# Attention products turned from features to tokens: exponentials split in two fp32r parts, attention stage unrolled

## What is computed

```python
def _fox_prompt_attention(q, k, v, logf):
    ...
        s = jnp.einsum('bqhd,bkhd->bhqk', q_i, k).astype(jnp.float32) * ATTN_SCALE
        s = s + cq_i[..., :, None] - ck[:, :, None, :]
        ...
        p = jax.nn.softmax(jnp.where(mask, s, -jnp.inf), axis=-1)
        return jnp.einsum('bhqk,bkhd->bqhd', p.astype(v.dtype), v)
...
            q, k_p, v_p, g, logf_p = _fox_project(yp, norm1_g, w_in1, fox_b_f, q_norm_g, k_norm_g)
            att = _fox_prompt_attention(q, k_p, v_p, logf_p)
            yp = yp + (att * jax.nn.silu(g)) @ w_out1
```

## Time and profile before

| | us |
|---|---|
| median of three runs | 3478.22 (3470.8 to 3479.21) |
| the profiled execution | 3480.33 |
| its span from first to last instruction | 3478.7 |
| PE busy, share of the span | 3017.1 (87%) |
| DVE / ACT / POOL busy | 1533.7 / 1032.3 / 761.5 |

### The profile page before, as it was taken

One profiled execution on the slowest core, in us unless ns is written; L12 is line 12 of the kernel. 1 busy time (PEld: TensorE's weight loads), 2 busy tenths in 40 slices (PEclk: granted clock), 3 DMA queues, 4 the chain that ended last, 5 costly groups with the idle time before them and its releaser, 6 DMA issues. The chain is left out here.

```text
span 3478.7 us, 48124 instructions
## 1 busy us (share of the span) xinstructions
PE 3017.1 (87%) x17005; PEld 2320.1 (67%) x17005; DVE 1533.7 (44%) x2068; ACT 1032.3 (30%) x1711; POOL 761.5 (22%) x475
## 2 busy tenths in 40 slices
PE   3879797959989999989996689898989889899799
PEld 3869696947759999989886445454545445454687
DVE  5132323233557667685775334343424333342332
ACT  5222223232452122221211234343434343343100
POOL 0000000010004886878765200000100000000000
PEclk9989898979989999999998799999999999999899
DMA  3111000035636888888785765748475757654442
GB/s 113 32 35 39 25 30 25 24 101 178 184 115 210 271 267 276 265 260 269 252 271 159 167 183 137 205 114 250 99 228 127 215 150 200 173 143 152 149 127 68
DMA packets 323904, 547.04 MB, mean 157 GB/s; under 512 B 77309, under 2 KB 221345, under 8 KB 314220
## 3 DMA queue, kind: packets, MB, share of 16 engines
q1 hardware_dynamic: 220172, 445.81, 42.8%
q10 hardware_dynamic: 95424, 75.61, 7.6%
q0 software_dynamic: 8128, 23.33, 2.1%
HBM read 449.58 MB, written 95.12 MB: 157 GB/s over the span
## 5 line engine op out<-in xcount | busy, mean ns | idle before, releaser
L1151 POOL TENSOR_TENSOR p_kp<-p_kp,p_qb 128x1024 f32<-128x1024 f32 x256 | 625.7, 2471 | 385.7 <-DMA p_kp<-in_cache_k_dram 314.0
L2076 DVE TENSOR_REDUCE at_mx<-at_mx 128x1 f32<-128x512 f32 (+3 forms) x640 | 379.9, 608 | 718.3 <-PE at_mx L1953 475.7
L2040 ACT ACTIVATE at_w<-at_st,c_nckt 128x512 f32<-128x512 f32 (+3 forms) x640 | 397.3, 623 | 690.9 <-PE at_st L1977 380.2
L1990 PE MATMUL at_o<-at_w,at_v 128*65 128x512 f32 (+3 forms) x1280 | 578.0, 535 | 17.0 <-DVE at_og L2086 8.0
L112 PE MATMUL p_pb<-p_w,x_xh 128*128 128x256 f32 x2048 | 591.8, 289 | 0.7 <-DVE p_w L1462 0.7
L113 PE MATMUL p_pb<-p_w,x_xh 128*128 128x256 f32 x2048 | 579.1, 283 | 0.0
L114 PE MATMUL p_pb<-p_w,x_xl 128*128 128x256 f32 x2048 | 578.6, 283 | 0.0
L1975 PE MATMUL at_st<-at_q,at_k 128*128 128x512 f32 (+3 forms) x640 | 407.4, 637 | 4.4 <-ACT at_w L2040 4.4
L1564 DVE TENSOR_REDUCE p_sc<-p_kp 128x16 f32<-128x1024 f32 x256 | 307.5, 1214 | 217.6 <-POOL p_kp L1151 217.3
L112 PEld LDWEIGHTS p_pb<-p_w,x_xh 128*128 128x128 f32 x2048 | 390.5, 191 | 12.1 <-issue 11.2
L113 PEld LDWEIGHTS p_pb<-p_w,x_xh 128*128 128x128 f32 x2048 | 391.9, 191 | 0.0
(11 more groups left out here) (289 smaller groups left out, 3880.4 us busy)
## 6 DMA issues: line engine op xcount, KB each, us to landing
p_kp<-in_cache_k_dram SPq DMA_DIRECT2D x256, 512.0 KB, 4.9
at_vp<-in_cache_v_dram SPq DMA_DIRECT2D x256, 512.0 KB, 5.6
o_mt<-mixed SPq DMA_DIRECT2D x32, 512.0 KB, 5.1
p_raw<-in_w_in_dram SPq DMA_DIRECT2D x32, 512.0 KB, 6.9
at_q<-qh SPq DMA_DIRECT2D x32, 512.0 KB
at_k<-kh SPq DMA_DIRECT2D x32, 512.0 KB
l_raw<-in_w_in_dram SPq DMA_DIRECT2D x20, 512.0 KB
mixed<-l_w POOLq DMA_DIRECT2D x8, 1028.0 KB, 4.2
```

Source lines behind the costliest of these rows:

```text
L1151: nc.gpsimd.tensor_tensor(kp[:, g % 4], kp[:, g % 4], qb[:], ALU.mult).then_inc(kmul, 1)
L1990: nc.tensor.matmul(O[0:HR, P * j:512], V[s][:, kb, :], W[n % 3][:, 0:512 - P * j], start=(kb == 0), stop=(kb == 4 * c + 3)).then_inc(pv, 1)
L2040: nc.scalar.activation(W[n % 3][:, 0:wd], ST[n % 2][:, 0:wd], ACT.Exp, bias=C.nckt[:, kb, ds(2 * i + u // NC, 1)]).then_inc(ex, 1)
L2076: nc.vector.reduce_max(mx[:, u % 2, j, seg:seg + 1], MX[m % 2][:, 0:wd], AX.X).then_inc(mread, 1)
```

## The change

1. In `attention` PV is turned: the exponentials become the stationary side, in tiles of 128 keys by 128 queries, and the values the moving side. Both are split in a high and a low fp32r part. For each tile there are two products: the high part with 130 columns (`V` high, two columns of ones, `V` low), and the low part with the first 66. At a unit's start a product with a row of zeros clears each half of `o`.
2. Between exponential and PV ACT rounds `w` to `wh` (RD), and POOL in two steps of three, DVE in the third, subtract for `wl` (WL). PV stands three steps behind its QK, further at a unit's start. `w` has four buffers, `wh` and `wl` five. The values of a head are split by ACT and POOL (VS).
3. The result lies by tokens. OE is on DVE alone, in two halves: reciprocal, four multiplications with division and gate, an addition. SP stores it; the gate is loaded by tokens, for each unit.
4. The maxima row goes through the `mx` tiles; `mr` is gone. The loop is gone: all 640 steps are written out, and waits are for constants.
5. In `project1` the gate isn't turned but stored by tokens, and the turn of a unit comes after the second next unit, `turn(n - 2)`.
6. In `out1` the division is gone; PE turns the tile of tokens by eight transposes, and ACT and DVE split it from PSUM.

```diff
             def turn(n):
...
-                if n and UNITS[n - 1][2] != "v":
-                    turn(n - 1)
+                if n >= 2 and UNITS[n - 2][2] in "qk":
+                    turn(n - 2)
...
+    VW = 2 * HD + 2
+    LAG = 3
+    RW, RH = 4, 5
...
+    def low_on_dve(n):
+        return n % 3 == 2
...
+        for h in range(2, H):
+            start = first_step(NC * (h - 1)) + 2
+            for x in range(NLD):
+                loads.setdefault(start + x, []).append(("LD", h, x))
+            loads.setdefault(start + NLD, []).append(("LV", h))
+            loads.setdefault(start + NLD + 9, []).append(("VS", h))
...
+            for x in range(NLD):
+                head_load(0, x)
             sp.dma_start(pt[:], a["page_table"]...).then_inc(pt_in, 16)
+            value_load(0)
+            gate_load(0)
+            gate_load(1)
             scores(0)
             sp.wait_ge(snz, 1)
             sp.dma_start(sn[0:1], ...).then_inc(sn_in, 16)
+            for x in range(NLD):
+                head_load(1, x)
+            sp.wait_ge(pt_in, 16)
+            value_group(0, 0)
+            value_group(0, 1)
+            value_load(1)
...
+            def value_low(h):
+                pool.wait_ge(vhd, h + 1)
+                nc.gpsimd.tensor_tensor(V[h % 2][:, :, LO], Vr[:], V[h % 2][:, :, HI].bitcast(F32), ALU.subtract).then_inc(vld, 1)
...
-                        nc.tensor.matmul(O[0:HR, P * j:512], V[s][:, kb, :], W[n % 3][:, 0:512 - P * j],
-                                         start=(kb == 0), stop=(kb == 4 * c + 3)).then_inc(pv, 1)
+                    for jj in range(j, 4):
+                        if kb == 0 and u and jj % 2 == 0:
+                            pe.wait_ge(osc, 2 * u - 1 + jj // 2)
+                        if kb == 0 and jj % 2 == 0:
+                            nc.tensor.matmul(O[:, jj // 2, 0:2 * VW], identr[0:1, :], zero[:], start=True, stop=False)
+                        q = slice(P * (jj - j), P * (jj - j + 1))
+                        nc.tensor.matmul(o_tile(jj, ALL), Wh[n % RH][:, q], V[s][:, kb, ALL], start=False, stop=False)
+                        last = nc.tensor.matmul(o_tile(jj, FRONT), Wl[n % RH][:, q], V[s][:, kb, FRONT], start=False,
+                                                stop=jj % 2 == 1 and kb == 4 * c + jj)
...
+            def value_high(h):
+                act.wait_ge(vr_in, 16 * (h + 1))
+                if h >= 2:
+                    act.wait_ge(pv, first_step(NC * (h - 1)))
+                nc.scalar.activation(V[h % 2][:, :, HI], Vr[:], ACT.Copy).then_inc(vhd, 1)
+
+            value_high(0)
+            value_high(1)
...
+                    nc.vector.reciprocal(ol[:, u % 2, 2 * half:2 * half + 2], one).then_inc(old, 1)
...
+                    for part, dst in ((HI, oa), (LO, ob)):
+                        for j in js:
+                            last = nc.vector.scalar_tensor_tensor(out=dst[:, j, :], in0=o_tile(j, part), scalar=ol[:, u % 2, j:j + 1],
+                                                                  in1=SG[u % 2][:, j, :], op0=ALU.mult, op1=ALU.mult)
+                    last.then_inc(osc, 1)
...
-                    last = nc.tensor.matmul(rb[:, n % 2, k, 0:rows], expand[:, k * P:(k + 1) * P], rl[:, ds(col, rows)],
-                                            start=True, stop=True)
+                    last = nc.tensor.transpose(tp[:, n % 2, k, :], mt[:, n % 3, k * P:(k + 1) * P], C.ident[:])
```

More of the change, by code:

```diff
@@ L1680, in attention, with blocks, first_step, width @@
     HR = HD + 1
-    NS = 2 * sum(4 * (c + 1) for c in range(NC))
-    NLD = 10
+    U = H * NC
+    HB = 2 * (NC * (NC + 1))
+    N = HB * H
+    NLD = 8
     VG = PG // 4
-    VI = PG // 4 + 1
+    VW = 2 * HD + 2
+    LAG = 3
+    RW, RH = 4, 5
+    def blocks(u):
+        return 4 * (u % NC + 1)
+    def first_step(u):
+        return HB * (u // NC) + sum(blocks(x) for x in range(u % NC))
+    def width(n):
+        u = max(x for x in range(NC * (n // HB), NC * (n // HB) + NC) if first_step(x) <= n)
+        kb = n - first_step(u)
+        return 512 - P * max(0, kb - 4 * (u % NC))
@@ L1848, in value_group, with values @@
                     page(vp[:, r % 2, g], a["cache_v"], PG * b + 4 * r + g).then_inc(v_in[r % 2], 16)
[L1850 to L1855 removed]
+            def values(b, r):
+                sp.wait_ge(vdone, (VG + 1) * b + r + 1)
                 if r < VG - 2:
@@ L1875, in _ @@
-            run(0, schedule(False), True, False)
-            with sp.Fori(1, B - 1) as i:
-                run(i, schedule(False), False, False)
-            run(B - 1, schedule(True), False, True)
+            due = []
+            for w in SEQ:
+                if w[0] == "LD":
+                    head_load(w[1], w[2])
+                elif w[0] == "LV":
+                    value_load(w[1])
+                elif w[0] == "OE" and w[2] == 1:
+                    due.append([3, w[1]])
+                elif w[0] == "SD" and w[-1] < B - 1:
+                    sp.wait_ge(sdd, 2 * w[-1] + 2)
+                    scores(w[-1] + 1)
+                elif w[0] == "VG":
+                    values(w[-1], w[1])
+                elif w[0] == "VN":
+                    values(w[-1], VG)
+                elif w[0] == "QK":
+                    for d in due:
+                        d[0] -= 1
+                    while due and due[0][0] <= 0:
+                        u = due.pop(0)[1]
+                        store(u)
+                        if u + 2 < U:
+                            gate_load(u + 2)
@@ L2159, in out1, with by_feature @@
         block = ctx.enter_context(nc.Block())
+        def by_feature(n, rows):
+            return tp[:, n % 2, :, :] if rows == P else ms[:]
         @block.sync
```

785 lines of the change are left out of this document (400 added, 385 removed).

## The result

| | before | after |
|---|---|---|
| median | 3477.53 us (4 runs) | 4064.57 us (4 runs, 4039.69 to 4078.92) |
| ratio, with its 95% interval | | 1.1685 (1.1625 to 1.1745) |
| the profiled execution | 3480.33 | 4078.92 |

What follows compares the result with a forecast made beforehand. PE was taken to bound attention, its clock falling to 1.2 GHz in even heads. 3480.3 + 461 (eight pairs) + 32 (start) + 3 (end) - 37 (project1) - 24 (out1) = 3915 us, range 3540 to 4010.

Steps and rivals of the forecast that it cites:

- PV's price: Attention: 0.11 us a product, 0.22 a tile at full clock, loads setting the price; +26 us at full clock.
- faster: Rival: loads overlap and a PV product costs less than 0.11 us; below 0.093 the kernel is faster; chance 0.05.
- Even heads: Attention: clock falls in unit c = 0 and stays at 1.2 GHz; 119.5 us a head, +53.6.
- Odd heads: Attention: groups of values bring the clock back each time; +4 us a head (0 to 12).
- the last chain: End of attention: the last blocks pass one more chain of exponential, rounding and subtraction; +3 us.
- the odd heads stay low too: Rival: a group of values at the low clock doesn't bring it back; 33 us more each, 4170; chance 0.08.
- The clock returns in part: Rival: clock returns by c = 1's steps or for half of the even heads; about 3700 us; chance 0.15.
- Project1: project1: 32 gate turns go, -13 us, and waits for a turn's rows shrink; -37 us in all (-13 to -50).
- The start: Start of attention: loads and the split of head 1's values delay the first QK to about 1992; +32 us (10 to 45).
- Out1: out1: inversion, spread and division go, eight transposes a tile come; -24 us.
- The chain: Attention: exponential, rounding, subtraction and hand-overs behind QK, some 4.3 us over three steps; 2.5 us a head at full clock.
- The clock stays up: Rival: c = 0 costs only one low stretch as before, a busy queue restoring the clock; 3552 us; chance 0.18.

Runs made afterwards that it cites:

- a5_low_130: Changed kernel with all 130 columns instead of 66 in the second product of each PV tile, no further load: 4033.62 us.
- e1_no_values: Changed kernel with seven of the eight groups of page values of each sample cut to one product of 8 columns: 4121.36 us.
- d2: Changed kernel with all but the first four pages of cached keys in project1 loaded with 128 of 1024 columns: project1 927.9 us, whole kernel 4077.86.
- d4: Changed kernel with GpSimd's multiplications of cached keys cut from 1024 columns to 64: project1 835.4 us, whole kernel 3978.67.
- a4: Changed kernel with the split of head 1's values on ScalarE and GpSimd moved from the stage's start to step 12: 4013.21 us.
- d3: Kernel before the change with GpSimd's multiplications of cached keys cut from 1024 columns to 64: project1 861.2 us, whole kernel 3429.15.
- a1_rows128: Changed kernel with operands of the second score product and the maxima product filled from 65 rows to 128: 3784.68 us.

## Why the prediction was wrong in size

**PV's price: right.** 0.22 and 0.44 us a tile were forecast from the earlier trace rows, 0.22 and 0.43 measured; a5_low_130 shows that the load is what counts. With this the rival "faster", which needed products under 0.093 us, falls.

**Even heads: right in size, wrong in place.** 123.9 instead of 119.5 us, low from end to end, as forecast. But the prediction let the clock fall in unit c = 0, while PE waits for VectorE. Unit c = 0 took 9.3 us, forecast 9.5, and that is luck: the forecast was VectorE's time with PE waiting and under 5 us of its own work. In head 4 PE was busy 9.30 of 9.30 us with this work at the low clock, since the clock had fallen earlier. Windows of the changed kernel: unit c = 0 of head 4, a stretch in head 7, then the end of head 7 up to the first QK of head 8:

```profile
2447.20:2456.50 9.30, 9.30 (x36) 8.59 (x36) 5.74 (x19) 3.53 (x8) 3.52 (x3) 0.50 0.49 106
...
2842.70:2852.90 10.20, 10.20 (x46) 6.99 (x44) 1.98 (x3) 1.98 (x4) 2.78 (x2) 0.50 1.02 290
...
2873.40:2893.90 20.50, 20.25 (x151) 14.96 (x143) 9.56 (x26) 11.73 (x22) 8.24 (x9) 1.00 0.59 186
2893.90:2904.10 10.20, 9.68 (x27) 6.24 (x28) 1.54 (x3) 1.21 (x2) 1.50 (x1) 0.50 0.50 161
2904.10:2917.80 13.70, 13.54 (x105) 12.52 (x104) 4.73 (x7) 9.89 (x17) 6.50 (x5) 1.00 0.46 154
2917.80:2922.10 4.30, 4.30 (x22) 4.30 (x22) 0.64 (x2) 1.79 (x5) 1.91 (x2) 0.50 0.09 19
```

Before the last fall PE was busy 13.54 of 13.70 us, with the new PV and the scores, and no wait above 0.2 us. So the plain stream loses the clock by itself. Heads 1, 3 and 9 end in the same way: PE busy for at least 13.4 us of 13.6 to 13.7 at 1.00, and then the fall.

**Odd heads: the step that failed.** "Groups of values ... bring the clock back each time" was true (e1_no_values), but the prediction took it that the clock then stays. Between groups and after the last one the plain stream loses it again, as in the rows above, and the clock is low for a time even where a group runs: the stretch from 2842.70 to 2852.90 holds 16 records of one. The odd heads ran at 0.68 to 0.83. They grew by 15.8 us each instead of 4, 94 us more in all and the largest part of the miss; the even ones by 58.2 instead of 53.6 (37 us). Less the 3 us booked for the last chain, that is the stage's 128. The profiled execution was the slowest of four; by the odd heads of d2 and d4 (108.0 and 107.4 us) the excess is 75 or 70 us instead of 94, and still the largest part. The rival "the odd heads stay low too", 4170 us, named this with a chance of 0.08, and the truth lay a third of the way to it: 11.8 us a head above the forecast, where that rival has 33. (Eight times 33 makes its time 4179 and not 4170.) "The clock returns in part" (3700) looked for the clock in the even heads, where it never returned. Having argued that full queues don't bring the clock back, the text should have asked whether they keep it.

**Project1: the other failed step.** 37 us of gain were forecast, none came. The term took the waits for rows as free to go and the turns as time on the path. Both are so (26 us between d3 and d4), but VectorE is held by GpSimd, so that what PE saved at the turns it waited for at the weights: the waits for rows fell from 37.6 to 24.9 us, and those for weights rose from 3.9 to 29.4.

**The start: right in kind.** +22.9 us where 32 were forecast with a range from 10 to 45. The wait itself is worth 30 (a4), but the rest of the start is 7 us shorter than before. The values of head 1 were there at 1981, forecast 1984, as the timeline of ACT shows:

```profile
1981.35 1.06 ACT L2105 ACTIVATE at_v<-at_vr 128x1024 fp32r<-128x1024 f32 x1 [30.81 <-DMA at_vr<-out_v_prompt_dram]
1982.43 0.58 ACT L2131 ACTIVATE at_q<-at_mx 1x512 fp32r<-1x512 f32 x1
```

**Out1: right.** The pitch of a tile is 11.78 us instead of 13.08, -22.5 in all for -24. **The chain: right in that it doesn't bound**, 8 us of waits for the subtraction in the whole stage, where the text priced the chain at 2.5 a head for the full clock; at the low clock PE is slower than the chain. Less waiting for pages was forecast at 4 us a pair, and was 8.

**The rivals.** "The clock stays up" (3552) didn't come, and its reading of a busy queue is refuted by head 4: PE busy in 123.81 of 124.10 us, clock 0.50. The page of the Trainium skill that the prediction cited beside it, "TensorE: Matmul & The Clock Gate", says in its section "The HAM clock gate" that idle windows lower the clock and sustained activity releases it; a1_rows128 shows that the rows that products fill count too. Where the page is read as a busy queue, the trace disagrees, and the measurement decides.

What stays open: why the filled rows held the clock in some heads (0.91) and not in others (0.56) of one run, and what it is in the stream that the clock follows. That the rows filled count and the moving columns of short products don't is shown by one run each.

## What to carry to other kernels

Before a product is turned so that the large operand becomes stationary, count its loads: each product with a tile of 128 by 128 of its own cost 0.11 us in the mean at the full clock, whether 1, 66 or 130 columns moved, while 512 moving columns hid the load. Then ask whether the new stream would hold TensorE's clock by itself, in every stretch, not only in the one where it waits; products that used 65 of the array's rows took no longer when zeros filled them to 128. And before a wait is booked as gain, look for what the waited-for engine shares with others: the wait may only change its line.

## What the runs showed of the hardware that was not expected

- TensorE's clock stayed at 0.50 for a whole head of 124 us with PE busy all the time. Filling 65 rows to 128 in two of the products raised it to 0.80 over the stage; raising the moving columns of another from 66 to 130 did not lift it in the even heads.
- Leaving out products made the kernel slower: seven of eight groups of page values less, 4121 us in one execution, where the whole kernel took 4040 to 4079.
- 64 more moving columns in 2176 products were free (a5_low_130).
- VectorE's operation of 128 by 512 with two SBUF operands took 2.15 us in the mean where GpSimd multiplied beside it for 91% of its time, 1.38 where for 52%, and 0.70 where the multiplications were short. An eighth of the bytes of keys made the stage 32 us longer.
